# One inference step of a hybrid decoder: sums of complex products moved from VectorE to TensorE, and the end of the S5 layer put in another order

## The reference, cut to what matters

```python
h = rmsnorm(x)                                       # 64 groups of 16 channels, 64 complex states each
bu = einsum("blgh,gph->blgp", h, bbar)               # complex
state[l] = abar * state[l-1] + bu[l]                 # associative scan over tokens; samples: one step from h0
y = einsum(state_re, c_re) - einsum(state_im, c_im) + d * h
z = gelu(y)
x = x + (z @ w_ga) * sigmoid(z @ w_gb)
...
s = q . k * scale, masked to k_pos <= q_pos          # attention of layer 1
```

## Time and profile before

| | |
|---|---|
| time, median of 3 runs | 2537.57 us (2535.74 to 2539.46) |
| the profiled execution | 2535.47 us, its span 2533.5 us, mean granted clock 0.984 |
| PE busy | 2426.7 us, 96% |
| DVE busy | 1246.8 us, 49% |
| ACT busy | 544.0 us, 21% |
| POOL busy | 658.4 us, 26% |

### The profile page before, as it was taken

The page is one execution under the profiler, slowest core; times in us unless marked ns, Lnnn a source line. Parts: engine busy times, 40 slices in busy tenths (PEclk is TensorE's granted clock), DMA queues, the critical chain, the costliest instruction groups (busy, mean ns, idle before and its releaser), DMA issues.

```text
span 2533.5 us, 41245 instructions
## 1 busy us (share of the span) xinstructions
PE 2426.7 (96%) x16662; PEld 2357.6 (93%) x16662; DVE 1246.8 (49%) x2172; ACT 544.0 (21%) x1109; POOL 658.4 (26%) x373
## 2 busy tenths in 40 slices
PE   6679999999999999999999899999999999999998
PEld 6669999999999999999999766689999999999998
DVE  8995234343333343456433677755344343333336
ACT  4434122000000000022100367743100000000003
POOL 0005323223333223322332100043223322333220
PEclk9889999999999999999999999999999999999999
DMA  3146111111111111112347355211111111111101
GB/s 116 31 98 210 39 45 51 36 49 50 50 51 42 42 50 50 50 34 76 101 145 213 120 146 152 68 34 42 42 51 50 42 42 50 50 50 50 38 30 68
DMA packets 87283, 174.79 MB, mean 69 GB/s; under 512 B 33994, under 2 KB 49866, under 8 KB 87122
## 3 DMA queue, kind: packets, MB, share of 16 engines
q1 hardware_dynamic: 78210, 156.60, 19.7%
q10 hardware_dynamic: 8912, 15.79, 2.0%
HBM read 148.54 MB, written 21.46 MB: 67 GB/s over the span
## 4 chain that ended last, share of the span: by engine, by line
PE 86%; DVE 4%; ACT 3%; DMA 2%; issue 2%; SPq 2%; ACTq 1%; POOL 0%; DVEq 0%; POOLq 0%
PE pair L1695 83%; PE pair L2110 1%; DMA kpg<-cache_k 1%; PE pair L1861 1%; DVE nmx L1543 1%; ACTq L398 1%; PE pair L1853 1%; DVE wmix L1573 1%; DMA X<-x_t 1%; DVE acc L1040 0%; SPq L391 0%; DVE kpg L1040 0%; DVE stok L1136 0%; ACT act_hi L663 0%; ACT prob L974 0%
## 5 line engine op out<-in xcount | busy, mean ns | idle before, releaser
L1695 PE MATMUL pair<-act_hi,w_hi 128*128 128x344 f32 x3264 | 1048.9, 321 | 7.6 <-DVE w_lo L1040 4.2
L1695 PE MATMUL pair<-act_hi,w_lo 128*128 128x344 f32 x3264 | 1043.7, 320 | 0.0
L1695 PE MATMUL pair<-act_lo,w_hi 128*128 128x344 f32 x3264 | 1043.3, 320 | 0.0
L1695 PEld LDWEIGHTS pair<-act_hi,w_hi 128*128 128x128 f32 x3264 | 616.1, 189 | 8.6 <-DVE w_lo L1040 4.4
L1695 PEld LDWEIGHTS pair<-act_hi,w_lo 128*128 128x128 f32 x3264 | 615.6, 189 | 0.0
L1695 PEld LDWEIGHTS pair<-act_lo,w_hi 128*128 128x128 f32 x3264 | 614.2, 188 | 0.0
L597 POOL CAST w_hi<-w_raw 128x1024 fp32r<-128x1024 f32 x178 | 205.5, 1154 | 1518.1 <-issue 689.1
L600 POOL TENSOR_TENSOR w_lo<-w_raw,w_hi 128x1024 fp32r<-128x1024 f32 x178 | 436.1, 2450 | 32.1 <-POOL w_hi L597 32.1
L1040 DVE TENSOR_TENSOR gate<-pair,R 128x344 f32<-128x344 f32 x132 | 68.2, 516 | 611.2 <-PE pair L1695 611.2
L1040 DVE TENSOR_TENSOR X<-X,pair 128x344 f32<-128x344 f32 x528 | 259.1, 509 | 189.4 <-PE pair L1695 189.2
L1695 PE MATMUL pair<-hid_lo,w_hi 128*128 128x344 f32 x1056 | 338.6, 321 | 0.0
(11 more groups left out here) (248 smaller groups left out, 1853.2 us busy)
## 6 DMA issues: line engine op xcount, KB each, us to landing
w_raw<-w SPq DMA_DIRECT2D x180, 512.0 KB, 3.3
kpg<-cache_k SPq DMA_DIRECT2D x16, 512.0 KB, 5.8
vpg<-cache_v SPq DMA_DIRECT2D x16, 512.0 KB, 7.5
qd<-qt SPq DMA_DIRECT2D x28, 256.0 KB, 5.3
ublk<-x_b SPq DMA_DIRECT2D x8, 576.0 KB, 8.1
X<-x_t SPq DMA_DIRECT2D x3, 1376.0 KB, 9.6
vt<-stage ACTq DMA_DIRECT2D x8, 516.0 KB, 6.8
z<-zblk SPq DMA_DIRECT2D x32, 128.0 KB, 3.2
```

Source lines behind the costliest of these rows:

```text
L1695: return t_.matmul(out, lhsT, rhs, start=start, stop=stop)
```

## The change

**Sums on PE.** The two sums at the end of each half of `states` are gone: DVE writes the four products to `H` and to a new tile `E`, and PE accumulates all four, so each block of `outputs_s5` has 8 more products `E,G` of 127 columns. The samples' two sums are gone too: PE adds `hs` through a product with the identity into bank 7, and ACT's `samples` copies the bank to `hs`.

**Buffers.** `H` is one buffer, not two. So DVE waits, before it writes the first half of `H` of part q, for all outputs of part q-1 (`s5_y`, 8q), and ACT writes the samples' initial states (`initial`) after the same wait. `W`, `bpad`, `G`, `zblk` and others lie elsewhere.

**Order.** `powers(q)` stands one part earlier on DVE, and still waits for the outputs of part q-2. `kernels(q)` stands between the two halves of `inputs(q)` on PE. SP loads `TM` of part q before it stores `z` of part q-1. `Z` is loaded in four DMAs of two row blocks, the first behind part 1's stores, the second and third behind part 2's; ACT rounds blocks 0 to 3 ahead of the first GELU of part 3, and 4 and 5 between its two halves. Two weight tiles are loaded during part 2.

**Token order.** The tokens of each block of 128 are permuted, so that `z_high` and `z_low` write runs of 16 words in place of single words 8 apart. `x`, the positions, the mask tiles and the order of the results follow on the host; no instruction behind the GLU changes its shape.

```diff
 def states(q):
-                dve.wait_ge(s5_vsc, q + 1)
...
-                for x in range(2):
-                    tt(hs[:, x, pr, :], hs[:, x, pr, :], vsb[:, q % 2, :, x, :], ALU.add)
...
-                    c.add(tt(h_r, g0, cb, ALU.mult))
-                    c.add(tt(tw[:, 0], g1, sb_, ALU.mult))
-                    c.add(tt(h_i, g0, sb_, ALU.mult))
-                    c.step(tt(tw[:, 1], g1, cb, ALU.mult))
-                    c.add(tt(h_r, h_r, tw[:, 0], ALU.subtract))
-                    tt(h_i, h_i, tw[:, 1], ALU.add).then_inc(s5_h, 1)
+                    if q and m == 0:
+                        dve.wait_ge(s5_y, 8 * q)
+                    tt(H[:, 0, am, NS + 1:HW_], g0, cb, ALU.mult)
+                    v_.scalar_tensor_tensor(E[:, 0, am, :], g1, -1.0, sb_, ALU.mult, ALU.mult)
+                    tt(H[:, 1, am, NS + 1:HW_], g0, sb_, ALU.mult)
+                    tt(E[:, 1, am, :], g1, cb, ALU.mult).then_inc(s5_h, 1)
...
 # DVE's loop
+            powers(1)
             for q in range(PARTS):
                 states(q)
-                if q + 1 < PARTS:
-                    powers(q + 1)
                 if q + 2 < PARTS:
                     weights(q + 2)
                     angles(q + 2)
                     inputs(q + 2)
                 if q + 1 < PARTS:
                     sines(q + 1)
+                if q + 2 < PARTS:
+                    powers(q + 2)
...
 # PE, inputs(q)
-                if q:
-                    pe.wait_ge(s5_ti, 2 * q)
                 for m in range(2):
+                    if m:
+                        kernels(q)
+                    if q:
+                        pe.wait_ge(s5_ti, 2 * q - 1 + m)
...
+                t_.matmul(bank[7][:, 0:2 * PP * NS], lhsT=ident[:], rhs=hs[:, :, q * PP:q * PP + PP, :],
+                          start=True, stop=False, skip_group_check=True)
...
 # PE, outputs_s5(q)
+                if q:
+                    pe.wait_ge(s5_gelu, 8 * q)
...
                         for Gx, x in ((G_re, 0), (G_im, 1)):
-                            for g2 in range(2):
...
+                            for state, c0 in ((H[:, x, pi, 0:BW], 0), (E[:, x, pi, 0:NB - 1], NS + 1)):
+                                for g2 in range(2):
...
 # SP's loop, behind the even loads of TM
+                if q:
+                    sp.wait_ge(s5_gelu, 8 * q)
+                    for s in range(L):
+                        store_z(sp, q - 1, s)
+                    store_samples(sp, q - 1)
...
                 if q == PARTS - 1:
+                    sp.wait_ge(z_out, 144 * (PARTS - 2))
+                    sp.wait_ge(s5_g, 2 * PARTS)
+                    sp.wait_ge(s5_k, 2 * PARTS)
+                    sp.dma_start(Z[:, 2:4], z_k[:, 2:4]).then_inc(z_in[1], 16)
...
+                    sp.wait_ge(z_out, 144 * (PARTS - 1))
+                    sp.dma_start(Z[:, 4:6], z_k[:, 4:6]).then_inc(z_in[2], 16)
+                    sp.wait_ge(s5_gelu, 8 * PARTS)
                     for s in range(L):
                         store_z(sp, q, s)
...
 # ACT, part 3
+                if q == PARTS - 1:
+                    weight_high(0)
+                    weight_high(1)
...
+                    for k in range(0, 4):
+                        z_high(k)
                 gelu(q, 0, 4)
                 if q == PARTS - 1:
-                    act.wait_ge(s5_fin, 1)
-                    z_high(0)
-                    z_high(1)
+                    for k in range(4, 6):
+                        z_high(k)
+                    z_samples(0, 6)
                 gelu(q, 4, 8)
```

More of the change, by code:

```diff
@@ L295, in build @@
         s5_y, s5_gelu = sem("s5_y"), sem("s5_gelu")
-        s5_ti = sem("s5_ti")
-        z_in = [sem(f"z_in{i}") for i in range(3)]
+        s5_ti, s5_h0 = sem("s5_ti"), sem("s5_h0")
+        z_in = [sem(f"z_in{i}") for i in range(4)]
         t_in, z_out, ssm_out = (sem(x) for x in ("t_in", "z_out", "ssm_out"))
@@ L464, in _ @@
                     store_samples(sp, q)
[L465 to L469, removed]
+                    sp.wait_ge(s5_fin, 1)
+                    sp.wait_ge(s5_vsc, PARTS)
+                    sp.dma_start(d["ssm_p"], fin[:]).then_inc(ssm_out, 16)
+                    sp.dma_start(d["ssm_s"], hs[:]).then_inc(ssm_out, 16)
             sp.wait_ge(z_out, 144 * PARTS)
-            sp.dma_start(Z[:, 6:8], z_k[:, 6:8]).then_inc(z_in[2], 16)
-            sp.wait_ge(z_in[2], 16)
+            sp.dma_start(Z[:, 6:8], z_k[:, 6:8]).then_inc(z_in[3], 16)
+            sp.wait_ge(z_in[3], 16)
             for n in range(NC):
@@ L772, in kernel_out @@
                     act.wait_ge(s5_zero, 1)
+                else:
+                    act.wait_ge(s5_y, 8 * q)
                 for n in range(1, L, 2):
@@ L793, in _ @@
             turned(0)
+            initial(0)
+            kernel_copy(0)
             samples(0)
[L795 to L796 removed]
+            kernel_rows(0)
             def z_high(k):
[L798 to L800 removed]
+                act.wait_ge(z_in[k // 2], 16)
+                a.activation(by_step(act_hi[:, k, 0:SEQ]), by_place(Z[:, k, 0:SEQ]), ACT.Copy).then_inc(z_hi, 1)
             def z_samples(first, last):
[L803 removed]
+                act.wait_ge(z_in[2 if last <= 6 else 3], 16)
                 a.activation(act_hi[:, first:last, SEQ:T], Z[:, first:last, SEQ:T], ACT.Copy).then_inc(zs_hi, 1)
@@ L1307, in states @@
             def states(q):
[L1309 removed]
+                pr = slice(q * PP, q * PP + PP)
                 CB, SB = CBs[q % 2], SBs[q % 2]
[L1311 to L1317 removed]
                 dve.wait_ge(s5_sb, q + 1)
@@ L1866, in _ @@
             inputs(0)
-            kernels(0)
             for q in range(PARTS):
@@ L1871, in _ @@
                 outputs_s5(q)
-                if q + 1 < PARTS:
-                    kernels(q + 1)
             def glu(i, half, beside={}):
@@ L2238, in _, with token_order @@
             spread(4, 2)
+def token_order():
+    return np.arange(SEQ).reshape(KT, P // L, L).transpose(0, 2, 1).reshape(SEQ)
 def constants():
     f = np.float32
+    order = token_order()
+    tok = order[:P]
+    pattern = np.zeros((P, P), f)
+    masked = np.zeros((P, 64), f)
+    for q in range(P):
+        lower = 48 + q % 16 if q >= 64 else q
+        upper = q if q >= 64 else 111 + q % 16 if q % 16 else P - 1
+        pattern[lower, q] = 1
+        if q < P - 1:
+            pattern[upper, q] = 1
+    for r in range(P):
+        masked[r] = np.where(tok[64 * (r // 64):64 * (r // 64) + 64] > tok[r], f(-1e30), f(0))
+    masked[P - 1] = f(-1e30)
     nvec = np.concatenate([np.arange(NW), L * np.arange(NJ), L * NJ * np.arange(NI)]).astype(f)
@@ L2246, in constants @@
     inv = (f(500000.0) ** (-np.arange(0, ROT, 2, dtype=f) / f(ROT))).astype(f)
-    pos = np.concatenate([np.arange(SEQ), np.full(NS, NPG * PAGE)]).astype(f)
+    pos = np.concatenate([order, np.full(NS, NPG * PAGE)]).astype(f)
     ang = (pos[None, :] * inv[:, None]).astype(f).astype(np.float64)
     rows = p % 8
-    r64, k64 = (p % 64)[:, None], np.arange(64)[None, :]
     return {
@@ L2361, with in_order @@
     y = r["y_t"].T
+    def in_order(x):
+        out = np.empty_like(x[:SEQ])
+        out[order] = x[:SEQ]
+        return out[None]
     def states(x, n):
```

186 lines of the change are left out of this document (93 added, 93 removed).

## The result

The changed kernel takes 2548.74 us (median of 7 runs, 2545.18 to 2553.34); the kernel before, run beside it, 2534.51 us (7 runs, 2533.38 to 2539.46). The ratio is 1.005, with a 95% interval of 1.004 to 1.0059: 12.7 us slower by the ratio (the two medians are 14.2 us apart). The profiled execution took 2551.11 us, its span 2549.0, 15.5 longer than the one before. Of all executions reported here one fell in a slow state and is left out of its ratio: 7078.85 us, among twelve of the kernel with two edits together.

What follows compares the result with a forecast made beforehand. DVE sets the pace in S5 parts 0 to 2, then a chain of waits to PE's restart. Restart 2.9 later plus 2.1 half clock is 5.0, with hand-overs 5.5 us: 2537.57 + 5.5 = 2543.0, range 2534 to 2548.

Steps and rivals of the forecast that it cites:

- hand-overs: Several new waits between engines, each 0.1 to 0.3 us over what was given; took the sum from 5.0 to 5.5.
- Sums and new products: S5 layer: a half of `states` on DVE falls to 9.04 us; PE's `E` products add 0.87 us a block.
- The path: S5 loop: none of DVE's 12 us reaches the end of outputs 2; 8 go to `powers(1)`, the rest to waiting for outputs.
- The half clock of part 0: PE, idle 3.1 us before part 0's second half of inputs, runs at half clock: 2 us lost, once.
- The period: One part of the S5 loop takes 19.5 + 16.8 + 0.1 = 36.4 us, not the 35.4 of DVE alone.
- From outputs 2 to G: `TM` loads, stores, `Z` load, roundings, then PE's blocks: G, part 3's last GELU end, at 197.4, 3.3 us later.
- From G to the restart: Part 3's last GELU end to PE's restart behind `first_glu`: 29.4 less 0.3 us, restart at 226.5, 2.9 later.
- The clock behind it: PE idles over 5 us before its restart and then runs at half clock: 2.1 us lost.
- `Z` holds up the GELUs: Rival, chance 0.17: roundings stay at 1.97 or `Z` 2 to 3 lands late; +8 to +10 us, 2546.5.
- Clock kept: Rival, chance 0.22: PE stays hot in the loop or at the restart; +1 to +3 us, 2540.
- Faster: Rival, chance 0.11: the `E` products cost PE nothing, outputs stay 9.0, period 35.4; 2531 to 2533.

Runs made afterwards that it cites:

- two edits together: Changed kernel with part 3's GELUs ahead of the roundings of `Z` 2 to 5 and 12 unused products in PE's loop gap: 2532.51 us, ratio 0.9996.
- The run that changed only the restart's clock: Changed kernel with 26 unused identity products on PE between `first_glu` and the second pair of GLU units: 2544.87 us, ratio 1.0045.
- GELUs first: Changed kernel, but ACT does all GELUs of part 3 before it rounds row blocks 2 to 5 of `Z`: 2541.96 us, ratio 1.0033.
- `powers` back: Changed kernel with `powers(q+1)` back behind `states(q)` on DVE, `kernels(q+1)` behind part q's outputs, stores ahead of `TM` loads: 2536.21 us, ratio 0.9996.
- 26 products: Unused identity products behind `first_glu`: 2544.87 us alone on the changed kernel, 2540.18 us with GELUs ahead of roundings and 12 products in the loop gap.
- products in the gap: Changed kernel with 12 unused identity products on PE ahead of the second half of the inputs of parts 1 to 3: 2545.45 us, ratio 1.0042.
- `powers` back and 26 products: Changed kernel with `powers(q+1)` behind `states(q)`, part 3's GELUs ahead of roundings, 26 unused products behind `first_glu`: 2533.95 us, ratio 0.9988.
- stores split: Kernel with `powers` behind `states`, GELUs ahead of roundings, now `z` stores split between SP and ACT, 6 unused products for 26: 2524.44 us, ratio 0.996.

## Why the prediction was right or wrong

Slower it is, and by more than the 5.1 us to which a chance of 0.45 was given. The size was wrong: 2543.0 forecast, 2548.74 measured, 0.7 above the range. As a difference the miss is larger, 5.5 us forecast for 12.7, since more runs brought the kernel before down from 2537.57 to 2534.51. In the profiled executions it is 5.5 for 15.5: 5.8 of the missing 10.0 lie ahead of the restart and 4.7 behind it, less the 0.5 that the forecast had added for hand-overs. By its steps:

- **Sums and new products: right.** A half of states 9.1 (9.04), the `H` and `E` products of a block 2.02 (2.00).
- **The path: right.** DVE's 12 us reached nothing; `powers` waited for the outputs, and `states(3)` for outputs 2. With `powers` back in its place they reached DVE's end (174.4).
- **The half clock of part 0: right to expect, mis-sized.** Forecast 2 us. From 76.75 to the first block's end it cost 4.5: 0.7 on the inputs, 0.3, 1.6 on the samples and 1.9 on the block. Outputs 0 ended at 98.6, not 95.4: 2.5 of it the clock, the rest the branch below and a start 0.3 later.
- **The period: 0.65 short.** 37.05 for 36.4. The branch on PE is 17.4 (118.26 to 135.65) for 16.8: 0.2 each in the half of inputs and the identity product, the rest in the outputs. Twice, 1.3.
- **From outputs 2 to G: right,** 29.2 forecast and 29.2 measured. `TM` 5.15, stores and landing 7.0 for 6.7, the load 5.48 for 5.04, a rounding 1.0. What the forecast took from the Trainium skill ("SBUF — State Buffer", the box on cache lines under Door 1), that each access to a new line of 16 bytes pays, agrees with the trace: two roundings in runs of 16 words took 2.00, strided ones 3.94. The estimate of 4.4 for the load by the Trainium skill ("DMA: Bandwidth & Descriptors", anatomy of one DMA), whose figures are for DMAs that GpSimd issues, was too low: 5.48 measured, issued by SP.
- **From G to the restart: 1.3 short,** 30.4 for 29.1, nearly all in `X`, 13.96 for 12.75.
- **The clock behind it: the step that failed.** I counted one half-clock stretch of 2.1, wrote that PE never stops from there, and put all later clock losses at nothing. Behind the restart the span grew by 6.8. The stretch cost 3.0 (7.72 busy at 0.61). PE does stop later: behind its wait of 1.53 us at 403.3 the clock fell and cost another 1.5 (7.16 at 0.79), and near 1160 us some 3.4 were lost, for 1.1 at the same place before. The 3.0 are the restart's. The run that changed only the restart's clock had 7.2 us less span in the profiled execution but 3.9 in the median and 1.3 by the ratio, so it does not show that the rest follows from the restart, and the cause of the later drops stays open. "Never idled there" was not so either: before, PE waited 0.93 us for `X` at 223.56.

2.9 + 3.2 + 1.3 + 1.3 = 8.7 is the restart: forecast, outputs 0, two periods, and the way from G. With 6.8 behind it, 15.5.

The rival "`Z` holds up the GELUs" gave +8 to +10, near the restart's delay, but not by its mechanism: the roundings took 1.0, the load 0.4 more. Yet that `Z` stood ahead of the GELUs was the largest single cost ahead of the restart; putting the GELUs first gave 6.7 us back there, and 2.1 more by a warmer part 0. I had taken this wait for part of the path without asking what it bought. "Clock kept" was wrong at both places. "Faster" fell with the price of the `E` products.

What stays open: why executions of one kernel differ by up to 13 us (`powers` back, 2526.57 to 2539.99), and where, since only one of each has a trace; and the later clock drops (some 1150, 1430 and 1650 us), which come in most kernels with changing depth.

## What to carry to other kernels

Work taken off the bounding engine is worth what the next wait in its program lets through: here 11 us on DVE gave 0.1, 1.4 or 3.3 us at PE's restart, by where `powers`, the GELUs and the stores stood. After such a change look in the order for waits in front of what now ends last, and count a pause of PE by what runs cold behind it, not only by the pause. A filler that keeps PE warm must be sized for the gap in that kernel: 26 products saved 3.0 us of half clock in one order and held PE up by 4.3 in the next.

## What the hardware showed that was not expected

**The clock after equal pauses.** A half of `inputs` takes 1.97 us at full clock. After the same pause of 2.69 us PE's time order reads, in the kernel with products in the gap:

```profile
105.39 1.97 PE L1718 MATMUL pair<-ublk,RT 128*64 128x128 f32 x32 [2.69 <-DVE tw L1069]
```

and in the one with the GELUs first:

```profile
107.19 3.27 PE L1718 MATMUL pair<-ublk,RT 128*64 128x128 f32 x32 [2.69 <-DVE tw L1069]
```

A shorter pause can lose it too. In the kernel with the GELUs first, PE had run full products before a pause of 1.59 us and kept the clock:

```profile
185.78 0.50 PE L1883 MATMUL pair<-H,G_re 64*128 64x136 f32 x4 [1.59 <-ACT zblk L806]
```

and in the kernel with `powers` back and 26 products it had run the samples' 64 products of 8 columns and lost it:

```profile
108.05 2.04 PE L1839 MATMUL pair<-ublk,RT 128*64 128x8 f32 x64
111.67 0.83 PE L1884 MATMUL pair<-H,G_re 64*128 64x136 f32 x4 [1.58 <-ACT hs L780]
```

So the length of a pause alone did not tell. Up to and with PE's restart, the longest pause in these kernels that kept the clock was 3.46 us, and every one of 4.1 us or more lost it.

**A wait of 1.5 us, the same in fourteen kernels.** Some 170 us behind the restart PE waits 1.5 us for `std` in every kernel here. Behind it the clock fell in eight of them (a mean of 0.91 over 20 us) and stayed at 1.00 in six. Neither the clock at the restart nor the length of the wait, 1.51 to 1.53 us, tells them apart.

**Two DMA queues did not issue stores twice as fast.** In SP's and ACT's time order, 8 stores from SP alone (`powers` back, 26 products), then 4 each from SP and ACT (stores split):

```profile
190.50 5.35 SPq L404 DMA_DIRECT2D z<-zblk  x8
```

```profile
186.57 3.39 SPq L404 DMA_DIRECT2D z<-zblk  x4
```

```profile
186.58 3.43 ACTq L404 DMA_DIRECT2D z<-zblk  x4
```

That is 0.67 us a store from one queue and 0.85 from each of two, so eight stores take 3.4 us and not 2.7. The loads of `TM`, which both engines issue at once in the changed kernel, took 0.64 us each from SP and 0.68 from ACT.
